# Attention pipelines one unit deeper, with a fourth buffer and a new order of ScalarE's copies

## The reference

```python
def mem_xattn(x, mem, wq, wk, wv, wo):
    B, S, _ = x.shape
    M = mem.shape[1]
    q = (x @ wq).reshape(B, S, XATTN_HEADS, XATTN_DH)
    k = (mem @ wk).reshape(B, M, XATTN_HEADS, XATTN_DH)
    v = (mem @ wv).reshape(B, M, XATTN_HEADS, XATTN_DH)
    s = jnp.einsum('bshd,bmhd->bhsm', q, k).astype(jnp.float32) * (XATTN_DH ** -0.5)
    p = jax.nn.softmax(s, axis=-1).astype(v.dtype)
    o = jnp.einsum('bhsm,bmhd->bshd', p, v).reshape(B, S, D_MODEL)
    return o @ wo
```

## Time and profile before

| | |
|---|---|
| median of three runs | 2211.05 us |
| profiled execution | 2209.07 us |
| its span, first to last instruction | 2207.1 us |
| TensorE busy | 2042.6 us (93%) |
| VectorE busy | 1563.2 us (71%) |
| ScalarE busy | 1067.1 us (48%) |
| mean granted TensorE clock | 0.955 |
| weights and inputs read | 569.77 MB, 260 GB/s over the span |

### The profile page before, as it was taken

The page is one execution under the profiler, slowest core; times in us unless marked ns, Lnnn a source line. Parts: engine busy times, 40 slices in busy tenths (PEclk is TensorE's granted clock), DMA queues, the critical chain, the costliest instruction groups (busy, mean ns, idle before and its releaser), DMA issues.

```text
span 2207.1 us, 24071 instructions
## 1 busy us (share of the span) xinstructions
PE 2042.6 (93%) x9132; PEld 1581.0 (72%) x9132; DVE 1563.2 (71%) x1998; ACT 1067.1 (48%) x1090; POOL 60.3 (3%) x86
## 2 busy tenths in 40 slices
PE   8999989999899997999998988799999777899996
PEld 4566578888657575888887865588888664788885
DVE  2735478889745536888896355799999644888986
ACT  1201167677411012767772354377767332577773
POOL 0100000000000000000000000000000000000000
PEclk9999979999999997999998989799999998899998
DMA  9856169899885642989994501289889521699993
GB/s 406 334 212 273 71 227 361 333 359 360 305 356 211 235 190 89 362 326 358 370 359 168 195 35 39 105 324 350 329 326 351 196 77 46 239 350 341 363 353 126
DMA packets 49210, 574.60 MB, mean 260 GB/s; under 512 B 5056, under 2 KB 9152, under 8 KB 10688
## 3 DMA queue, kind: packets, MB, share of 16 engines
q1 hardware_dynamic: 34560, 500.19, 60.0%
q0 software_dynamic: 8352, 59.77, 6.7%
q10 hardware_dynamic: 6176, 12.97, 1.7%
HBM read 569.77 MB, written 3.15 MB: 260 GB/s over the span
## 4 chain that ended last, share of the span: by engine, by line
PE 69%; issue 17%; DVE 8%; DMA 3%; ACT 2%; POOL 0%; ACTq 0%; DVEq 0%; POOLq 0%
PE bank L767 66%; PE bank L797 2%; DVE ring_parts L1837 2%; DMA hi_ring<-in_ada 2%; DMA x<-in_x_in 1%; DVE work L1837 1%; ACT mix L1397 1%; DVE mix L1963 1%; ACT work L1397 1%; DVE hi_ring L2295 1%; DVE mix L1837 0%; ACT work_parts L1397 0%; DVE mix L2309 0%; DVE small L1837 0%; DVE small L1880 0%
## 5 line engine op out<-in xcount | busy, mean ns | idle before, releaser
L1837 DVE TENSOR_TENSOR ring_parts<-ring,hi_ring_parts 128x2048 fp32r<-128x2048 f32 x398 | 894.0, 2284 | 89.1 <-ACT hi_ring_parts L1397 87.9
L1397 ACT ACTIVATE hi_ring_parts<-ring 128x2048 fp32r<-128x2048 f32 x398 | 753.2, 1914 | 221.6 <-PE bank L767 121.4
L767 PE MATMUL bank<-hi_ring_parts,tokens 128*128 128x512 f32 x2048 | 662.8, 393 | 3.1 <-DVE mix L1837 1.7
L767 PEld LDWEIGHTS bank<-hi_ring_parts,tokens 128*128 128x128 f32 x2048 | 384.6, 188 | 85.0 <-DVE mix L1837 3.4
L767 PE MATMUL bank<-ring_parts,tokens 128*128 128x512 f32 x1024 | 399.0, 390 | 0.0
L767 PE MATMUL bank<-hi_ring_parts,work_parts 128*128 128x512 f32 x1024 | 326.4, 390 | 0.0
L1397 ACT ACTIVATE work<-bank 128x512 f32<-128x512 f32 (+6 forms) x207 | 108.6, 527 | 446.2 <-PE bank L767 434.1
L767 PEld LDWEIGHTS bank<-hi_ring_parts,work_parts 128*128 128x128 f32 x1024 | 192.2, 188 | 40.0
L767 PEld LDWEIGHTS bank<-ring_parts,tokens 128*128 128x128 f32 x1024 | 192.6, 188 | 37.6
L767 PE MATMUL bank<-ring_parts,work_parts 128*128 128x512 f32 x512 | 199.3, 389 | 0.0
L767 PE MATMUL bank<-ring,oT 128*128 128x512 f32 x384 | 166.1, 593 | 4.7 <-DVE oT L1993 2.4
(11 more groups left out here) (210 smaller groups left out, 1873.6 us busy)
## 6 DMA issues: line engine op xcount, KB each, us to landing
ring<-in_weights SPq DMA_DIRECT2D x238, 2048.0 KB, 8.4
hi_ring<-in_ada POOLq DMA_DIRECT2D x48, 1024.0 KB, 10.3
work<-in_vecs POOLq DMA_DIRECT2D x8, 1024.0 KB, 5.0
work<-bias_rows ACTq DMA_DIRECT2D x4, 1024.0 KB, 7.8
work<-in_memT_in ACTq DMA_DIRECT2D x2, 1024.0 KB, 13.4
bias_rows<-work ACTq DMA_DIRECT2D x8, 256.0 KB, 5.9
params<-in_prm ACTq DMA_DIRECT2D x1, 1389.5 KB, 12.9
consts<-in_cst ACTq DMA_DIRECT2D x1, 1040.0 KB, 18.6
```

What stands on the lines that cost most here:

```text
L767: ins = nc.tensor.matmul(o, lhsT, rhs, start=start, stop=stop)
L1397: return nc.scalar.activation(o, i, f, **kw)
L1837: return v.tensor_tensor(o, a, b, op)
```

## The change

The loops of the three engines get one step more. TensorE turns unit k-3 instead of k-2 and does the values of unit k-4 instead of k-3; VectorE's output copies go from k-3 to k-4; ScalarE's copies of turned probabilities go from k-2 to k-3 and stand ahead of the exponentials of unit k instead of behind them. `before_values` moves from step 3 to step 4; `between` stays in step 2. The probabilities get a fourth buffer, the first two of the eight chunks of `xT`, and are taken by the unit's number modulo 4. No operation is added or removed.

```diff
--- before.py
+++ after.py
@@ -378,9 +378,11 @@
 
         def aP(u):
 
-            i = u["n"] % 3
+            i = u["n"] % 4
             if i < 2:
                 return aP2[:, i, :, :]
+            if i == 3:
+                return xT[:, 0:2, :]
             return cut(work, EX + 3072 if u["name"][1] == "." else 12672, 2, S)
 
         aPT = cut(work, 13312, 2, 4, P)
@@ -881,23 +883,23 @@
 
             def attention(units, between=None, before_values=None):
                 n = len(units)
-                for k in range(n + 3):
+                for k in range(n + 4):
                     if k < n:
                         u = units[k]
                         product(u["name"] + ".s", [(a * S, a * S + u["nk"], P, u["scores"][a]) for a in range(2)])
                     if k == 2 and between:
                         between()
-                    if 2 <= k <= n + 1:
-                        u = units[k - 2]
+                    if 3 <= k <= n + 2:
+                        u = units[k - 3]
                         pe.wait_ge(att_prob, u["n"] + 1)
                         src = aP(u)
                         transposes(u["name"] + ".t", [
                             ((2 * a + kt) * P, (2 * a + kt + 1) * P, u["kp"], src[:, a, kt * P:kt * P + u["kp"]])
                             for a in range(2) for kt in range(u["tiles"])])
-                    if k == 3 and before_values:
+                    if k == 4 and before_values:
                         before_values()
-                    if k >= 3:
-                        u = units[k - 3]
+                    if k >= 4:
+                        u = units[k - 4]
                         if u["first"]:
                             begin(u["o"])
                         bank = psum[banks.jobs[u["o"]][0]]
@@ -1475,13 +1477,13 @@
                         carry(u["name"] + ".t", [(o[0:kp, 0:4:2, :],
                                                   lambda t: t[0:kp, :].rearrange("p (a b) -> p a b", a=4)[:, 0:4:2, :])])
 
-                for k in range(len(units) + 2):
+                for k in range(len(units) + 3):
+                    if k >= 3:
+                        turned_probs(units[k - 3])
                     if k < len(units):
                         exps(units[k])
                     if k == 2 and between:
                         between()
-                    if k >= 2:
-                        turned_probs(units[k - 2])
 
             def split_expert(tag, j, halves=(0, 1)):
 
@@ -1993,13 +1995,13 @@
                         drained(u["o"], v.tensor_copy(u["dest"], p_[:, 0:r * P].rearrange("p (a b) -> p a b", a=r)))
 
                 n = len(units)
-                for k in range(n + 3):
+                for k in range(n + 4):
                     if k < n:
                         biased_max(units[k])
                     if 1 <= k <= n:
                         normalise(units[k - 1])
-                    if k >= 3:
-                        outputs(units[k - 3])
+                    if k >= 4:
+                        outputs(units[k - 4])
 
             exps = [0]
```

## The result

The changed kernel takes 2190.19 us (median of six runs, 2185.88 to 2194.38), the kernel before 2211.73 us beside it (six runs, 2209.1 to 2217.92). The ratio is 0.9902, with an interval of 0.9887 to 0.9916: 21.5 us faster, where 16.4 us were forecast (2194.6 us, range 2188 to 2206). The profiled execution of the changed kernel took 2185.88 us with a span of 2184.0 us, 23.1 us less than the span before.

What follows compares the result with a forecast made beforehand. Attention was taken to be bound by a loop with VectorE waiting for scores, no engine full. Gains of 13.1 (even) + 4.0 (odd) - 0.7 (cross-attention) = 16.4 us gave 2194.6 us by the median, range 2188 to 2206.

Steps and rivals of the forecast that it cites:

- the loop: MoBA part: 5.14 us over two units through ScalarE's copy; after the change it covers three, 1.7 us each.
- The even layer: Even layer's attention: 14.9 + 0.7 us of VectorE waits, less 1.5 and 1.0 kept, gives a gain of 13.1 us.
- the fill: First NSA group of the even layer: of 3.5 us lost to waits, 1.5 us stay, TensorE being slow at half clock.
- single waits: Even layer: 1.0 us of waits remains where a wide score meets a short normalisation, an estimate of 0.2 us per part.
- The odd layer: Odd layer's attention: 7.2 us of waits, less 1.94 for the second unit's scores and 1.3, gives 4.0 us.
- MLA and low clock: Odd layer: 1.3 us of waits kept for MLA's TensorE work and low-clock stretches, chosen between 0 and 5.3.
- all waits gone: Both attention layers: if all waits went (15.6 + 7.2 us) and cross-attention cost nothing, 2188.2 us.
- Cross-attention: Two layers of four units, TensorE full: values(0) wait for copy(0), losing 0.35 us a layer, 0.7 us; bounds 0 and 1.2.
- cover of the copies: ScalarE's wait ahead of exps(k) is covered by VectorE's maximum: cost 0, bound 0.3 us x 22 narrow units = 7 us.
- A: Rival, both attention layers: low-clock stretches stay and keep waits, so the gain is 10.2 us, 2200.9 us; chance 0.25.
- B: Rival, self-attention: copies hold the exponentials and VectorE's normalisation stalls, leaving a gain of 3 us, 2208 us; chance 0.12.
- C: Rival: TensorE at 1.2 GHz through much of attention makes it slower, 2222 us at 70 us of low clock; chance 0.08.

Runs made afterwards that it cites:

- doubled outputs: VectorE's copy of the 28 biased outputs made twice: on the changed kernel 2196.75 us, on the kernel before 2213.87 us.
- the three runs above: Changed kernel with biased outputs copied twice, with the earlier cross-attention, and with three buffers, earlier cross-attention and ScalarE copying biased outputs: 2196.75, 2190.4, 2182.45 us.
- the old order: Changed kernel with the cross-attention of the kernel before put back, one unit less deep, copies behind the exponentials: 2190.4 us in one run.
- order alone: Kernel before with ScalarE's copies moved ahead of the exponentials, depth and three buffers unchanged, cross-attention as it was: 2202.47 us, ratio 0.9962.
- depth alone: Kernel before made one unit deeper with four buffers, ScalarE's copies still behind the exponentials: 2202.96 us, ratio 0.9959.

## Why the prediction was right, and where it was off

- **The mechanism.** The forecast that VectorE becomes the bound held: MoBA pair 3.73 us (forecast 3.8), undisturbed NSA group 11.09 (11.1), no listed waits up to the last maximum of the even layer but the first. The doubled outputs show it directly. The account of the loop was incomplete. The prediction read only ScalarE's copy, in the earlier trace rows; the trace of before also has TensorE waiting 5.8 us for normalisations, and of these 1.8 us are left, where the prediction had none left. It put three units between scores(k+1) and the maximum, which is right for the whole change; that the same loop of two units closes over the normalisation as well, so that the depth was needed for one loop and the order for the other, was seen only through the runs. That the change opens both was never worked out, and to that extent the sum for the even layer is luck.
- **The even layer, 13.1 forecast, 16.6 measured.** The mis-sized term is the fill: of the first group's 3.5 us of waits, 1.5 were kept because TensorE at half clock needs 18.2 us a group. In the profiled execution all of it went, with 2.8 us at the low clock instead of 6.7. Where the low clock lasted 6.7 us again (the three runs above) 1.1 us of wait stayed, so the term was near what such a stretch costs, and missed because the stretch was shorter. Another 1.0 had been kept for single waits: none came. The last 1.0 is no wait at all: up to the last maximum VectorE's busy time fell from 50.8 to 49.7 us, and the gaps outside the listed waits stayed at 5.7 and 5.8. One output copy of 0.28 us moved into the drain. The rest is overlap that a wait hides:

```profile
1330.75 0.69 DVE L1839 TENSOR_TENSOR xT<-xT,small 128x512 f32<-128x512 f32 x1
1331.36 0.28 DVE L1995 COPY oT<-bank 128x128 f32<-128x128 f32 x1
```

  In the changed kernel the copy starts 0.61 us after the scaling of 0.69 us ahead of it. Before, such a copy (1350.81 in the earlier trace rows) came 0.67 us after the scaling's end, so the wait cost 0.75 us and not 0.67.
- **The odd layer, 4.0 forecast, 6.7 measured.** The second unit's wait stayed, 1.61 us of 1.94, as forecast. The 1.3 us kept for MLA and low clock were not needed. MLA was to stay TensorE's at 4.6 us a pair; that step did not show, as VectorE waits for no score behind the second unit's, and the MLA part gained 1.5 us, 0.45 of them by an output copy that now comes later. VectorE's waits fell from 7.2 to 1.6, which is 5.6. Of the other 1.1, 0.7 are again busy time, a copy of 0.3 us moved into the drain among it, and 0.4 gaps outside the listed waits. A sum over listed waits is thus not an upper end: "all waits gone" gave 22.8 us for the two layers, and they gained 23.3.
- **Cross-attention, -0.7 forecast, -0.8 measured,** by the mechanism that was written down: +0.39 and +0.44 us, with a wait of 0.34 us ahead of values(0). The 12.08 us with the old order show it, in one trace with both layers; in time it can't be told apart.
- **Drain 0, buffer 0, cover of the copies 0 (bound 7 us).** All held. The drain is 7.12 us before and after, but as a sum of two: order alone makes it 6.63, depth alone 7.57. Up to the last maximum of the even layer ScalarE waits only for VectorE, and VectorE never for ScalarE, so the copies hold nobody up.
- **The rivals.** A, low-clock stretches stay: in the profiled execution they became shorter (mean clock of the even stretch 0.91 before, 0.97 after), and where one stayed as long it cost 1.2 us in the first group, where A had 4.0 more than the forecast over the even layer. The rule of the Trainium skill (TensorE: Matmul & The Clock Gate, "A second HAM failure mode: psum-queue depth-cycling") names the idle gaps between groups of matmuls: agreeing with it, TensorE idles 16.6 us of the even stretch before and 7.2 after, and the mean clock rises from 0.91 to 0.97. But two of the four NSA groups are at 1.00 in both, and order alone, with 12.8 us idle, has a lower clock (0.89). That shorter gaps raise the clock is thus not shown. B, the copies holding the exponentials: no such wait. C, TensorE at 1.2 GHz throughout: no. The three lines of what would be wrong (pair above 4.4, VectorE waiting for ScalarE at its reciprocals, mean clock below 0.85) did not come about; the one wait of 0.6 us for ScalarE, at the drain's reciprocal, is there before the change too.

## What to carry to other kernels

In a pipeline across three in-order engines, write down for each hand-over which instruction of the same queue must come first, and count the units that the ring spans: where several rings close over the same number of units they have to be opened together, or the next takes over. How much it takes over depends on how long its way is against the bound's own work: in the even layer either change alone brought 2.7 and 3.9 of 16.6 us, in the odd layer 4.6 and 5.6 of 6.7. To see them in a trace, read the waits of the engine in the middle by whom it waits for, not only those of the engine that should be the bound. Adding a known piece of work to the supposed bound, before and after, tells whether it is the bound more cleanly than taking something away.

## What the hardware showed beyond the forecast

- The stretches at the low clock fall in the same place of the same program: in two executions of the kernel before, both in the first and third group, with mean clocks of 0.75 and 0.78, then 0.74 and 0.78.
- Their price is not fixed: for the same 6.7 us at 1.2 GHz, the first group waits 3.5 us with the pipeline of before and 1.1 us with one unit more. That this is TensorE's stock of scores is argued, not shown.
- A listed wait understates what it costs: without one, an instruction starts 0.08 us before the end of the scaling ahead of it (1331.36 above).
